# A two-block network in float32r products: the columns of every weight product are walked in 32 pieces instead of in one run

## What is computed

```python
# first block
h = swiglu(rmsnorm(x, norm_ffn1_pre), w_ffn1_in, w_ffn1_out)      # 1024 -> 2*2816 -> 1024
x = x + 0.5 * rmsnorm(h, norm_ffn1_post)
h = mixer(rmsnorm(x, norm_mix_pre), w_mix_in, ..., w_mix_out)     # convolution and mLSTM, both directions
x = x + rmsnorm(h, norm_mix_post)
h = swiglu(rmsnorm(x, norm_ffn2_pre), w_ffn2_in, w_ffn2_out)
x = x + 0.5 * rmsnorm(h, norm_ffn2_post)
# second block
h = rms_norm(x, norm_gain) * (1 + scale) + shift                  # shift, scale, gate from silu(c) @ w_ada
q, k, v, z_a, u, z_b, m_a, m_b = split(h @ w_in)                  # 8 parts of 1024
p_a = (stick_breaking_attention(q, k, v) * silu(z_a)) @ w_branch_a
p_b = (multiscale_causal_pool(u) * silu(z_b)) @ w_branch_b
out = (sigmoid(m_a) * p_a + sigmoid(m_b) * p_b) @ w_out
return rms_norm(x + gate * out, final_gain)
```

## Time and profile before

| | |
|---|---|
| three timed runs | 1655.81, 1655.87, 1656.45 us (median 1655.87) |
| profiled execution | 1659.67 us |
| its span, first to last instruction | 1658.0 us |
| mean granted TensorE clock | 0.977 of full |
| PE busy | 1588.6 us, 7173 matmuls |

### The profile page before, as it was taken

One profiled execution on the slowest core, in us unless ns is written; L12 is line 12 of the kernel. 1 busy time (PEld: TensorE's weight loads), 2 busy tenths in 40 slices (PEclk: granted clock), 3 DMA queues, 4 the chain that ended last, 5 costly groups with the idle time before them and its releaser, 6 DMA issues.

```text
span 1658.0 us, 18823 instructions
## 1 busy us (share of the span) xinstructions
PE 1588.6 (96%) x7173; PEld 1282.3 (77%) x7173; DVE 806.7 (49%) x890; ACT 589.8 (36%) x775; POOL 210.3 (13%) x218
## 2 busy tenths in 40 slices
PE   7999999997999998999999998899999999999997
PEld 6888888885777886888888887777777778788876
DVE  4333335325455745533334334677777766432244
ACT  5222213224455423422222223555656543222132
POOL 4555555004000002000000001000000000000001
PEclk9999999997899998999999998899999999999998
DMA  5444444230121221332232222112121223323321
GB/s 185 156 133 150 144 146 147 81 101 26 51 72 56 76 103 51 102 101 89 89 101 101 99 78 76 51 52 76 51 76 51 63 90 102 96 82 101 101 76 51
DMA packets 135383, 150.68 MB, mean 91 GB/s; under 512 B 3104, under 2 KB 123036, under 8 KB 135340
## 3 DMA queue, kind: packets, MB, share of 16 engines
q1 hardware_dynamic: 131580, 137.40, 26.2%
q0 software_dynamic: 3616, 12.65, 2.5%
q10 hardware_dynamic: 144, 0.04, 0.0%
HBM read 147.98 MB, written 2.10 MB: 91 GB/s over the span
## 4 chain that ended last, share of the span: by engine, by line
PE 82%; DVE 6%; ACT 5%; issue 3%; POOL 2%; DMA 0%; SPq 0%; DVEq 0%; ACTq 0%; POOLq 0%
PE ps L1542 25%; PE ps L1544 25%; PE ps L1543 25%; ACT wh L584 2%; DVE Gc L1325 1%; POOL xT L523 1%; PE ps L1822 1%; PE ps L1741 1%; DVE acc L1024 1%; ACT be L811 1%; PE ps L1603 1%; PE ps L1832 1%; PE ps L1831 1%; POOL acc L517 1%; PE ps L1711 0%
## 5 line engine op out<-in xcount | busy, mean ns | idle before, releaser
L1542 PE MATMUL ps<-ah,wh 128*128 128x512 f32 x1504 | 606.0, 403 | 14.6 <-DVE al L1016 9.3
L1544 PE MATMUL ps<-ah,wl 128*128 128x512 f32 x1504 | 591.4, 393 | 0.0
L1543 PE MATMUL ps<-al,wh 128*128 128x512 f32 x1504 | 590.6, 393 | 0.0
L983 DVE TENSOR_TENSOR wl<-raw,wh 128x2048 fp32r<-128x2048 f32 x94 | 215.3, 2291 | 406.1 <-ACT wh L584 405.7
L584 ACT ACTIVATE wh<-raw 128x2048 fp32r<-128x2048 f32 x110 | 210.6, 1915 | 490.2 <-PE ps L1544 490.0
L1542 PEld LDWEIGHTS ps<-ah,wh 128*128 128x128 f32 x1504 | 286.2, 190 | 79.3 <-issue 18.5
L1544 PEld LDWEIGHTS ps<-ah,wl 128*128 128x128 f32 x1504 | 285.0, 189 | 61.5
L1543 PEld LDWEIGHTS ps<-al,wh 128*128 128x128 f32 x1504 | 285.8, 190 | 54.4
L1544 PE MATMUL ps<-rh,wl 128*128 128x512 f32 x352 | 139.1, 395 | 0.0
L1542 PE MATMUL ps<-rh,wh 128*128 128x512 f32 x352 | 139.0, 395 | 0.0
L1543 PE MATMUL ps<-rl,wh 128*128 128x512 f32 x352 | 139.0, 395 | 0.0
(11 more groups left out here) (283 smaller groups left out, 1685.1 us busy)
## 6 DMA issues: line engine op xcount, KB each, us to landing
raw<-in_w_ffn_in SPq DMA_DIRECT2D x43, 1024.0 KB, 5.0
raw<-in_w_ffn_out SPq DMA_DIRECT2D x22, 1024.0 KB, 4.9
raw<-in_w_in SPq DMA_DIRECT2D x36, 512.0 KB, 5.0
raw<-in_w_in SPq DMA_DIRECT2D x14, 1024.0 KB, 5.9
ada_raw<-in_w_ada POOLq DMA_DIRECT2D x24, 512.0 KB, 4.3
raw<-in_w_mix_in SPq DMA_DIRECT2D x10, 1024.0 KB, 5.2
raw<-in_w_mix_out SPq DMA_DIRECT2D x4, 1024.0 KB, 4.9
raw<-in_w_branch_a SPq DMA_DIRECT2D x4, 1024.0 KB, 5.0
```

Of the source, the lines that this page charges most:

```text
L983: nc.vector.tensor_tensor(wl[n % 2][:], raw[n % 2][:], wh[n % 2][:].bitcast(fp32), ALU.subtract).then_inc(lo_done, 1)
L1542: nc.tensor.matmul(bank, w[0], m[0], start=start, stop=False)
L1543: nc.tensor.matmul(bank, w[0], m[1], start=False, stop=False)
L1544: return nc.tensor.matmul(bank, w[1], m[0], start=False, stop=stop)
```

## The change

A view `woven` is put on the accumulator and on both moving tiles at the head of `three`. The 512 columns, which were walked 0, 1, ..., 511, are now walked 0-15, 256-271, 16-31, 272-287, ..., 240-255, 496-511: 32 pieces of 16 columns (64 bytes), alternating between the lower and the upper half of the same 2048 bytes. As both sides are walked in the same order, each column's sum is written where it was. Weight slices, the number and order of instructions on every engine, the waits, the tiles and their addresses are as before. Lines from here on stand 5 lower in the changed kernel (1542 becomes 1547).

```diff
         @block.tensor
         def _(pe):
+            def woven(ap):
+
+                return ap.rearrange("p (h c e) -> p c h e", h=2, e=16)
+
             def three(bank, w, m, start, stop):
 
+                bank, m = woven(bank), (woven(m[0]), woven(m[1]))
                 nc.tensor.matmul(bank, w[0], m[0], start=start, stop=False)
                 nc.tensor.matmul(bank, w[0], m[1], start=False, stop=False)
                 return nc.tensor.matmul(bank, w[1], m[0], start=False, stop=stop)
```

## The result

The changed kernel takes 1713.59 us (median of four runs, 1708.66 to 1713.95) against 1655.84 us (median of four, 1650.77 to 1656.45): the ratio is 1.0353, with a 95% interval of 1.0331 to 1.0375. The profiled execution took 1713.65 us. The forecast was 1612 us as the likeliest, in a range of 1568 to 1700: the sign was wrong, and the middle missed by 101 us.

What follows compares the result with a forecast made beforehand. It took PE's products in `three` to bound the kernel. Whole loss 92.5 less 5.1 us in waits is 87.4; half, 43.7, off the profiled 1659.67 gives 1616.0, or 1612.2 us at the runs' median; range 1568 to 1700.

Steps and rivals of the forecast that it cites:

- What bounds the kernel: Products on PE in `three`: their start-to-start price decides the time, 226.7 ns with `ah`/`al`, 233.3 with other tiles.
- 5.1 us of a change: Attention rounds: about half of a 10.3 us change over 768 products is swallowed by waits for ACT and DVE.
- the moving read and the weight load get in each other's way: PE's two address streams in `three`: their collision causes part of the loss, 13.4 or 20.0 ns a product.
- one delay can set them apart: Moving read in `three`: at half pace it advances like the weight load, winning nothing up to the whole loss, 92.5 us.
- I take half of it, 43.7 us: All products of `three`: half of the 87.4 us whole loss is recovered, no row being nearer to either bound.
- my signs of being right: Product starts in the changed kernel: closer than 226.7 and 233.3 ns, 426 at the lower clock, tile prices nearer each other.
- The second part, PSUM at no cost: Accumulator write in `three`: jumps taken as free by VectorE's rows, bounded at 26.7 ns a product, 163 us in all.
- The cheap tiles become dear: Products on `ah`/`al`: the new walk raises them from 226.7 to 233.3 ns, +27 us, 1683 us; chance 0.12.
- Each piece costs: Every break of the walk restarts reader or writer: 13.3 ns a product, 1732 us, or 1809 with two cycles; chance 0.23.
- Nothing changes: Products of `three`: the loss has nothing to do with column order; 1655.9 us, within 3.3 us; chance 0.20.

Runs made afterwards that it cites:

- e5: Kernel before with `ah` and `al` moved up by 128 bytes, weights kept at their offset: ratio 1.0108, 1672.4 us against 1655.3.
- e6: Kernel before with 384 bytes of padding below the tiles of the phases (`rh`, `yh`, `gah`, `dh` and their partners): ratio 0.9954, 1646.3 us against 1655.3.
- e9: Kernel before with the weights `wh` and `wl` moved up by 128 bytes, moving tiles left at their offsets: 1665.9 us against 1651.4.
- e11: Changed kernel with the moving tiles at five other distances from the weights (0, 64, 192, 256, 384 bytes): 1708.2 us.
- e14: Changed kernel with the second matmul of three loading 64 weight columns instead of 128: 1713.8 us against 1652.0 of the kernel before.
- e13: Kernel before with both sides in pieces of 16 columns, all even pieces first, then all odd ones: 1713.1 us against 1652.0.
- e7: Kernel before, plain walk, with the second matmul of three loading 64 weight columns instead of 128: 1660.5 us.
- e15: Kernel before with both sides woven in four pieces of 128 columns, 512 bytes each: 1656.9 us against 1652.0.
- e16: Kernel before with both sides woven in 8 pieces of 64 columns, 256 bytes each: 1655.4 us against 1655.6.
- e17: Kernel before with the moving read in pieces of 16 columns, each 320 bytes after the last, four of them eight times over; accumulators in one run: 1651.4 us against 1655.6.
- e3: Kernel before with both sides woven in 16 pieces of 32 columns, 128 bytes each: 1690.6 us against 1652.4.
- e4: Kernel before with both sides woven in 64 pieces of 8 columns, 32 bytes each: 1724.6 us against 1652.4.
- e8: Kernel before with every matmul of `three` reading the first 32 columns of its moving tile 16 times, accumulators in one run: 1699.7 us against 1655.3.
- e18: Kernel before with the moving read in repeated pieces of 16 columns, each beginning 256 bytes after the last; accumulators in one run: 1712.3 us against 1655.6.
- e2: Kernel before with only the accumulators woven in 32 pieces, moving tiles in one run: 1654.0 us against 1652.4.
- e10: Kernel before with the moving tiles at distances 0, 64, 192, 256 and 384 bytes from the weights: 1650.4 us against 1651.4.
- e12: Kernel before with the moving tiles at distances 32, 96, 160, 224 and 480 bytes from the weights: 1676.8 us against 1652.0.

## Why the prediction was wrong

- **What bounds the kernel** held. Products set the time, and the loss per product was there to be changed, by tile, as read from the starts. I had 5.1 us of a change go into waits, all in attention. The waits took 7.7 us: some 3.5 us in the eight attention rounds (an estimate from five of them), some 2 us in the mixer, which I had left out, and the rest elsewhere. That about half of a change in attention is swallowed held (0.44 of 0.74 us a round). What I had wrong there is the price: 226.7 ns was read from dense stretches and used for the attention's products, which stood 231 ns apart.
- **That the moving read and the weight load get in each other's way, depending on where the tiles lie**, held: `e5`, `e6` and `e9` show that the distance between the two addresses sets the price of a plain walk. My remark that the dearer tiles also lie higher up is of no account.
- **The step that failed** is the one behind "the moving read jumps 1024 bytes every 16 columns ... it advances at half its pace, closer to that of the weight load. If both streams advance alike, one delay can set them apart, and they stay apart", and with it the term "I take half of it, 43.7 us". The walk at half pace lost 32 cycles a product instead of 16 or 24, at every distance from the weights (`e11`) and with half the load beside it (`e14`). The even-then-odd walk, at double pace, lost the same 32 (`e13`). So pace by itself was not the matter. Nor is it likely that the two streams failed to advance alike: 64 weight columns fewer shortened the load's row from 188 to 134 ns (`e7`), which makes 0.84 ns a weight column of 4 bytes, an estimate, and the low bits of the woven read advance 4 bytes per 0.83 ns. By that they went alike, and the loss grew. The term of 43.7 us off stands against 53.9 us added.
- **What the runs showed in its place:** what counts is that the low eight bits of the moving address come in their natural order: then jumps are free (`e15`, `e16`, `e17`), otherwise 28 to 36 cycles go (`e3`, `e4`, `e8`, `e13`, `e18`). One of my signs of being right, that the prices of the two kinds of tile come together, came true, but at 240 ns: it says nothing for the mechanism.
- **The second part, PSUM at no cost**, held (`e2`), though VectorE's rows were weak evidence for it: TensorE takes 512 columns 3.1 times as fast (226.7 ns against 692), not 2.5 times. The Trainium skill's rule that PSUM access which is not contiguous slows matmuls significantly ("SBUF — State Buffer", section "Door 1: The DMA port swizzle") does not show in pieces of 64 bytes: 226.7 and 233.3 ns, as in one run. The Trainium skill's statement of two independent read ports for columns and weights ("TensorE: Matmul & The Clock Gate", section "Step-by-step: what each phase is for") can't be the whole story: the distance between the two sets 226.7 or 233.3 ns.
- **The rivals.** "The cheap tiles become dear" had the kind of cause right, a walk that collides worse, but stopped at 233.3 ns and 1683 us; the dear tiles became dearer too. "Each piece costs" comes nearest in time, with 1732 us. Its 13.3 ns a product give 240.0 ns on `ah`, as measured, but 246.6 on `rh`, which has 240.0; and it is wrong as a mechanism: `e17` has as many breaks and pays for none. "Nothing changes" is out.
- **What stays open** is what in the chip has this period of 256 bytes; why a load of half the columns makes the plain walk on `ah` dearer; why products on `ah` stand further apart in attention; and whether the 32 cycles of the woven walk are a matter of the weight load at all. Neither its place (`e11`) nor its length (`e14`) changed them, two other walks that break the order do depend on the tile (`e8`, `e18`), and no run here was without the load.

## What to carry to other kernels

Where float32r products run back to back at the high clock, read the step between starts per moving tile. If tiles have different prices, look at their addresses modulo 256 bytes against the weights': aligning them alike took 6.7 ns off each of 1584 products and 0.46% off this kernel, for one padding line. Leave the moving columns in one run, or in pieces of 256 or 512 bytes that jump by multiples of 256, and if a layout needs pieces, it is the moving side that must keep the order; the accumulator side can be walked in pieces of 64 bytes for nothing.

Before a bet on a mechanism in the memory, ask for the run that shows the two sides apart: here `e2` and `e9` would have said more than the whole trace.

## What the runs showed of the hardware

- A float32r matmul of 512 columns, in a dense stretch at the 2.4 GHz level and on the mean of three, takes 226.7 ns from start to start when moving tile and weights are 0 or 256 bytes apart modulo 512 (kernel before, `e10`), 228.7 at 64 (`e10`), 232.3 to 233.3 at 128 (kernel before, `e5`, `e9`) and 233 to 234.3 at 32, 96, 160, 192, 224, 384 and 480 (`e10`, `e12`). Between other work of PE, in attention, it was 231 ns at a distance of 0. At the 1.2 GHz level it is 427 ns, one column a cycle, in both kernels.
- Walking the moving columns in pieces of 8, 16 or 32 that break the order within 256 bytes costs 243.3, 240.0 and 236.6 ns (`e4`, the changed kernel, `e3`). Thirty-one jumps that keep it cost nothing (`e17`).
- Walking the accumulator in 32 pieces of 64 bytes costs nothing (`e2`).
- A load of 64 weight columns instead of 128 has a row of 134 ns instead of 188. It made products on `ah` dearer (229.8 ns), left those on `rh` at 233.3 in the mean (`e7`), and left the woven walk at 240.0 (`e14`).
